# A weight unit's low part: GpSimd's two subtractions of 128x512 become four of 128x256

## What is computed

```python
def hybrid_layer(x, positions, norm_mix, w_in, conv_w, w_conv_out, ret_norm, w_ret_out, w_o, norm_mlp, w_up, w_down):
    h = rmsnorm(x, norm_mix)
    proj = h @ w_in
    cb, cc, cu, q, k, v, g, ga, gb = jnp.split(proj, split_points, axis=-1)
    y_conv = short_conv_mixer(cb, cc, cu, conv_w, w_conv_out)
    y_ret = retention_mixer(q, k, v, g, positions, ret_norm, w_ret_out)
    merged = jax.nn.sigmoid(ga) * y_conv + jax.nn.sigmoid(gb) * y_ret
    x = x + merged @ w_o
    h2 = rmsnorm(x, norm_mlp)
    return x + jnp.square(jax.nn.relu(h2 @ w_up)) @ w_down
...
def second_block(...):
        z = rms_norm(x, mix_norm_g[l]) @ w_in[l]
        ...
        x = x + y @ w_out[l]
        x = x + memory_cross_attention(...)
        x = x + conv_ffn(x, ffn_norm_g[l], ffn_w_up[l], ffn_dw_w[l], ffn_dw_b[l], ffn_w_down[l])
    return rms_norm(x, final_norm_g)
```

## Time and profile before

| | |
|---|---|
| median of 3 runs | 2584.31 us (2584.26 to 2587.22) |
| the profiled execution | 2588.98 us, its span 2587.2 us |
| TensorE busy | 2526.8 us, 98% of the span |
| GpSimd busy | 1256.5 us, 49%, of which line 437 1250.1 us |
| VectorE busy | 1204.6 us, 47% |
| ScalarE busy | 912.7 us, 35% |
| granted TensorE clock | 0.99 of full speed as a mean |

### The profile page before, as it was taken

The page is one execution under the profiler, slowest core; times in us unless marked ns, Lnnn a source line. Parts: engine busy times, 40 slices in busy tenths (PEclk is TensorE's granted clock), DMA queues, the critical chain, the costliest instruction groups (busy, mean ns, idle before and its releaser), DMA issues.

```text
span 2587.2 us, 34387 instructions
## 1 busy us (share of the span) xinstructions
PE 2526.8 (98%) x11744; PEld 2046.3 (79%) x11744; DVE 1204.6 (47%) x1407; ACT 912.7 (35%) x1307; POOL 1256.5 (49%) x879
## 2 busy tenths in 40 slices
PE   8999999999999999999999999999998799999998
PEld 7887788888888888878888888878755587888887
DVE  6444612452322542453145322257667544788363
ACT  5223433332222322343233222233367433444233
POOL 5555355555555454524555555545322243555454
PEclk9999999999999999999999999999999999999999
DMA  5332233333333333323333333363211131333332
GB/s 161 98 97 82 65 98 98 98 92 98 96 96 98 99 95 95 95 66 90 96 94 95 98 98 98 98 147 91 74 50 50 49 90 53 94 98 97 98 96 76
DMA packets 444025, 236.24 MB, mean 91 GB/s; under 512 B 16145, under 2 KB 438161, under 8 KB 443793
## 3 DMA queue, kind: packets, MB, share of 16 engines
q1 hardware_dynamic: 442800, 232.38, 31.2%
q10 hardware_dynamic: 1120, 2.51, 0.3%
HBM read 232.76 MB, written 2.10 MB: 91 GB/s over the span
## 4 chain that ended last, share of the span: by engine, by line
issue 44%; POOL 34%; PE 20%; DVE 1%; POOLq 1%; ACT 0%; ACTq 0%; DVEq 0%
POOL wl L437 34%; PE unit_ps L1861 14%; PE unit_ps L1847 3%; PE aux L2118 1%; PE unit_ps L2084 1%; PE unit_ps L2178 0%; PE aux L2136 0%; POOLq L435 0%; PE o_banks L2084 0%; POOLq L310 0%; DVE rstd L1695 0%; DVE x L1223 0%; DVE d L1494 0%; PE o_banks L2128 0%; DVE cl L1575 0%
## 5 line engine op out<-in xcount | busy, mean ns | idle before, releaser
L437 POOL TENSOR_TENSOR wl<-raw,wh 128x512 fp32r<-128x512 f32 x862 | 1250.1, 1471 | 1310.6 <-ACT wh L514 832.7
L514 ACT ACTIVATE wh<-raw 128x1024 fp32r<-128x1024 f32 x304 | 322.5, 1061 | 1030.8 <-PE unit_ps L1740 962.2
L1740 PE MATMUL unit_ps<-ah,wh 128*128 128x512 f32 x1280 | 502.2, 392 | 0.0
L1740 PE MATMUL unit_ps<-ah,wl 128*128 128x512 f32 x1280 | 498.2, 389 | 0.0
L1740 PE MATMUL unit_ps<-al,wh 128*128 128x512 f32 x1280 | 498.0, 389 | 0.0
L1740 PE MATMUL unit_ps<-bh,wh 128*128 128x512 f32 x768 | 299.7, 390 | 0.0
L1740 PE MATMUL unit_ps<-bl,wh 128*128 128x512 f32 x768 | 298.8, 389 | 0.0
L1740 PE MATMUL unit_ps<-bh,wl 128*128 128x512 f32 x768 | 298.8, 389 | 0.0
L1740 PEld LDWEIGHTS unit_ps<-al,wh 128*128 128x128 f32 x1280 | 240.4, 188 | 51.4 <-issue 1.9
L1740 PEld LDWEIGHTS unit_ps<-ah,wh 128*128 128x128 f32 x1280 | 240.3, 188 | 51.3 <-issue 1.9
L1740 PEld LDWEIGHTS unit_ps<-ah,wl 128*128 128x128 f32 x1280 | 240.3, 188 | 49.8
(11 more groups left out here) (375 smaller groups left out, 3840.3 us busy)
## 6 DMA issues: line engine op xcount, KB each, us to landing
raw<-w_in_dram SPq DMA_DIRECT2D x147, 512.0 KB, 4.0
raw<-w_up_dram SPq DMA_DIRECT2D x64, 512.0 KB, 4.0
raw<-w_down_dram SPq DMA_DIRECT2D x64, 512.0 KB, 3.7
raw<-up_dram SPq DMA_DIRECT2D x44, 512.0 KB, 3.8
raw<-w_conv_out_dram SPq DMA_DIRECT2D x16, 512.0 KB, 3.7
raw<-w_ret_out_dram SPq DMA_DIRECT2D x16, 512.0 KB, 3.6
raw<-w_o_dram SPq DMA_DIRECT2D x16, 512.0 KB, 3.7
raw<-down_dram SPq DMA_DIRECT2D x16, 512.0 KB, 3.8
```

The lines of the kernel that those rows point to most:

```text
L437: last = pool.tensor_tensor(wl[j][:, half], raw[j % 2][:, half], wh[j][:, half].bitcast(F32), ALU.subtract)
L514: act.activation(wh[j][:], raw[j % 2][:], ACT.Copy).then_inc(w_hi, 1)
L1740: last = pe.matmul(unit_ps[j % 2][:], w[j][:, k], v[:, k * T:(k + 1) * T], start=(k == 0 and n == 0), stop=(k == KB - 1 and n == 2))
```

## The change

The two subtractions of a unit, over four blocks each, are issued as four over two blocks each. The numbers that are computed are the same. The semaphore `w_lo` is raised by the last of them as before; nothing else in the program changes.

```diff
             def body(u, j):
                 pool.wait_ge(w_hi, u + 1)
-                for half in (slice(0, KB // 2), slice(KB // 2, KB)):
-                    last = pool.tensor_tensor(wl[j][:, half], raw[j % 2][:, half], wh[j][:, half].bitcast(F32), ALU.subtract)
+                for k in range(0, KB, 2):
+                    pair = slice(k, k + 2)
+                    last = pool.tensor_tensor(wl[j][:, pair], raw[j % 2][:, pair], wh[j][:, pair].bitcast(F32), ALU.subtract)
                 last.then_inc(w_lo, 1)
```

## The result

Four pieces a unit take 2589.68 us as the median of 22 runs (2588.33 to 2592.3); the kernel before took 2586.10 as the median of 22 in the same comparison. The ratio is 1.0014 with a 95% interval of 1.0008 to 1.0021, +3.6 us (+2.1 to +5.4). The forecast was +4.0 us, within what was called the same. Its absolute number, 2588.3, rested on three runs of before with a median of 2584.3; more runs put that at 2586.1. All medians here are of undisturbed runs; one of 11 runs of the quiet kernel with four pieces, which took 5682.56 us, is left out.

The account below looks back on a forecast made before the run. TensorE was taken as the bound, except in the first 50 us and about 1740 to 2170 us. 3.6 + 0.5 + 0.4 - 0.5 = +4.0 us on the median 2584.3 gave 2588.3 us, range 2584.8 to 2592.5.

Parts of the forecast that it names:

- The hidden part: Units after the first 41 us: +0.30 us a unit where VectorE is away, up to +1.7 beside it, at price 0.
- The start: First 41 us, where the chain runs through GpSimd and the DMAs: stepped to +3.8, bounds +1.2 to +6.8, taken as +3.6 us.
- "+1.2" for unit 0: First microseconds: unit 0 gets two VectorE instructions in place of part of one and is done at 13.9, 1.2 us later.
- the light start: Rival, 24%: at the start GpSimd often gets two pieces in a row, or only the 0.30 counts; 2585.9 us.
- +2.7: First microseconds: unit 1, with about four VectorE instructions, ends at 19.1, 2.7 us later in all.
- unit 3, then its buffer's DMA, then unit 5: Chain at the start: unit 3 ends +3.5 us late, unit 5 +3.8, then unit 7's DMA and copy, then the square root.
- +0.5 at 1740.87: TensorE's wait for VectorE at 1740.87, four contending instructions beside one unit: 0.5 us longer.
- +0.4 at 1957.47: TensorE's wait for VectorE at 1957.47, seven taps with a subtraction inside: 0.4 us longer.
- The third, -0.5: TensorE's wait for VectorE at 2068.11, where lone contending instructions come sooner: 0.5 us shorter.
- The ring: Rival, 9%: raw buffers become the bound where VectorE is dense, once a subtraction passes 5.8 us; 9 us in the FFN, 2597.
- Slower by denser handovers: Rival, 11%: in the attention, +2 us or more on top of 4.0, so +6, 2590.3 us.
- The faster one: Rival, 6%: shorter port holds free VectorE where TensorE waits for it, 1740 to 2170 us; -10.8 against the start's +3.6, 2577.

Follow-up runs that it names:

- the quiet kernel with four pieces: Against the kernel before: VectorE's early low parts wait for unit 1's subtraction, its sums of squares for unit 3's; units 0 to 7 in four pieces; 2588.27 us, ratio 1.0012.

## Why the prediction was right, and where its steps were wrong

**The hidden part** was right. A lone unit was to cost 2.85 us and takes 2.82 (355 us and after, in the changed kernel's timeline: `360.92 2.82 POOL`), the FFN's was to take 3.9 and takes 3.80, and TensorE is busy for all of 2300 to 2350. Four pieces outside the start cost nothing (-0.4 us with an interval of 2.3).

**The start** was right as the place, and in size: +3.6 forecast, +3.1 and +2.5 in two traces, +3.5 us timed alone. The path that gave this number was wrong, so the hit is in part luck. The prediction read unit 0's 2.71 us off the chain of work, which leaves out the end of its last piece; the timeline has 3.02 before (9.97 to 12.99) and 3.7 after (9.71 to 13.45). The "+1.2" for unit 0 is +0.7 by its length, and this also takes away what spoke for the light start, that VectorE hardly slowed unit 0. Unit 1 ended at 18.02, +1.6 and not +2.7, and TensorE's wait there is 1.55 us and not 2.6; unit 3 ended at 26.9, +1.8 and not +3.5.

Above all the chain does not run "unit 3, then its buffer's DMA, then unit 5". Unit 5's subtraction waited for unit 4's, and unit 4 came from the DMA that unit 2's end releases. Along that path: unit 2 ends 0.9 us later (22.60 for 21.74), the DMA of unit 4 up to its copy takes 6.73 us in place of 5.50 (22.63 to 29.36), 1.2 more, and units 4 and 5 together take 6.76 in place of 5.58, 1.2 more, since VectorE's angle computations, which I had not counted as contending, run beside them and now get more turns. That is +3.3 at the end of unit 5. The 1.2 of the DMA belong more likely to this execution than to the change: in the trace of four pieces at the start alone it took 5.60, units 4 and 5 together took 7.42, and the wait ended 2.5 later.

**The steps that failed** in the attention are two of the three waits of the earlier trace rows. "Where it has a dense run, each of four pieces is put between, 4 x 0.65 less a part of the first, in place of 2 x 1.27 less a part" gave +0.5 at 1740.87 and +0.4 at 1957.47. Measured at the second place: 0.3 shorter, and the dense run itself 0.74 us shorter where I had it longer. At the first place the 1.75 us of the kernel before were chance: seven other traces with two pieces there have 0.71 to 0.92, so the 0.85 after is no change, and the +0.5 did not come. The third, -0.5, measured -1.0.

The error is the equation of a piece's duration with the time for which it keeps VectorE out. In a dense stretch before, VectorE's instructions of 0.69 us took 1.60 and started 1.69 apart; after, they take 1.04 and start 1.15 apart, and 1.04 is also what `al` takes in the FFN of the changed kernel (L914 of before, L915 and L1650 after; ns min/median/max):

```profile
L914 DVE TENSOR_TENSOR d<-d x7: 674/1594/1607, 18.2 to 26.6; 128x512 f32<-128x512 f32 x7
...
L915 DVE TENSOR_TENSOR d<-d x7: 1037/1043/1208, 17.4 to 24.4; 128x512 f32<-128x512 f32 x7
...
L1650 DVE TENSOR_TENSOR al<-tmp,ah x14: 683/1044/1047, 2241.2 to 2516.7; 128x512 fp32r<-128x512 f32 x14
```

With one piece a turn, 1.69 - 0.69 = 1.00 us is left for a 128x512 piece, of which two alone start 1.25 apart, and 1.15 - 0.69 = 0.46 for a 128x256 piece (0.70 apart alone). So some 0.24 us of each piece cost VectorE nothing. Four pieces keep it out for 4 x 0.46 = 1.8 us, two for 2.0; with full durations I had 2.6 and 2.5. The sign of these terms hung on that.

**The rivals.** The light start (24%) did not come. The ring did not come even with eight pieces. "Slower by denser handovers" had the wrong sign for the waits. The faster one, "the shorter hold of the port frees VectorE", had the right mechanism and was too small with four pieces; with eight in the right 44 units it makes -6.9 us. It was given 6% and priced only as a whole with the start's loss.

**Is the gain in the attention real, when each kernel was traced once?** The 14 traces can be read together, by the number of pieces in units 304 to 347. The waits are those of TensorE for VectorE at the three places; a stretch goes from the end of one wait to the end of another, and the middle mark is the wait for the compressed scores (`c_f`):

| pieces | traces | waits, us | first wait to `c_f` | `c_f` to third wait | both |
|---|---|---|---|---|---|
| two | 8 | 0.71 to 0.92, once 1.75; 4.37 to 4.39; 7.35 or 7.36 | 127.0 to 132.2 | 195.1 to 197.0 | 324.0 to 327.5 |
| four | 2 | 0.85; 4.06; 6.28 and 6.32 | 133.0 and 133.9 | 193.1 and 192.4 | 326.1 and 326.2 |
| eight | 4 | 0.31 to 1.68; 2.97 or 2.98; 5.85 or 5.86 | 129.8 to 132.4 | 187.0 to 190.7 | 319.4 to 320.4 |

Eight pieces make the whole stretch some 4 to 8 us shorter in every pair of traces, which agrees with the times. Four pieces shorten the second part by 2 to 5 us and give nothing over both, which agrees with the 0.4 us by the clock of the runs: the first part is longer in both traces than in any with two pieces.

**What stays open** is why. Between 1780 and 1820 us TensorE's granted clock is 0.91 and 0.96 of full speed in the two traces with four pieces, and 1.00 in six of the eight with two, 0.96 in the other two. Whether the pieces bring the lower clock, or two executions happened to have it, two traces don't tell.

## What to carry to other kernels

Splitting an instruction on a port that two engines share moves time from one to the other; ask stage by stage which of the two is waited for. Where TensorE waits for VectorE, GpSimd's pieces should be small (eight pieces: -6.9 us); where the chain goes through GpSimd, as in filling the pipeline, they should be large (four: +3.5, eight: +7.0); in between no difference showed within the interval. A median of "no change" can be a loss at one place that hides a gain at another, and the same edit limited to a range of units tells them apart.

## What the runs showed of the hardware

Alone, GpSimd's two-input subtractions of 128x512 start 1.25 us apart, those of 128x256 0.70 and those of 128x128 0.42 (350 to 400 us, in the kernels with two, four and eight pieces everywhere), so some 0.14 us an instruction don't shrink.

The Trainium skill says that whichever side starts first gets the shared port for the whole instruction and the other blocks ("SBUF — State Buffer", section "SBUF: two separate sides"). The traces here agree only nearly: in a dense run VectorE loses 1.00 us of a piece's 1.25, 0.46 of 0.70, and 0.18 of 0.42 (its instructions start 0.87 apart there), about 0.24 us less than the piece each time.
